# Filling products of ones in front of waits of TensorE, in a two-layer hybrid backbone on one NeuronCore

## What is computed

```python
# layer 0, state-space heads: both directions, chunkwise scan with scalar decay
y, ss_f, ss_b = bidir_scan(ch, bh * dt[0], bh * dt[1], xh, log_a[0], log_a[1], init[2], init[3])
y = y + xh * d_skip[None, :, None, None]
y = y.transpose(0, 2, 1, 3).reshape(b, l, SSD_INNER) * jax.nn.silu(z)
y = rmsnorm(...)                               # then concatenated, @ w_out
# layer 1, mLSTM
den = jnp.sum(s, axis=-1) + w_inter * jnp.einsum('bhid,bhd->bhi', qc, n0)
h = num / jnp.maximum(jnp.abs(den), jnp.exp(-m_row))[..., None]
```

## Time and profile before

| | us |
|---|---|
| median of 3 runs | 2368.23 |
| lowest and highest of them | 2364.69, 2372.87 |
| the profiled execution | 2359.82 |
| its span, first to last instruction | 2358.1 |
| busy in it: PE, DVE, ACT, POOL | 2274.4, 1370.9, 905.6, 1058.7 |
| mean granted clock of TensorE | 0.987 |

### The profile page before, as it was taken

How to read it: one execution, slowest core, us unless ns; L and a number is a source line. 1 busy time by engine, 2 the same in 40 slices (tenths; PEclk the granted TensorE clock), 3 DMA queues, 4 the chain that set the end, 5 groups by cost and what they waited for, 6 DMA issues and landing times.

```text
span 2358.1 us, 32703 instructions
## 1 busy us (share of the span) xinstructions
PE 2274.4 (96%) x11907; PEld 1962.0 (83%) x11907; DVE 1370.9 (58%) x1750; ACT 905.6 (38%) x1979; POOL 1058.7 (45%) x815
## 2 busy tenths in 40 slices
PE   7999999999879999999999999999999999999998
PEld 5999999998537999999999998976555568888887
DVE  5995788764666456856857456653568654111113
ACT  5215435443793256756746252132221213101002
POOL 3353334334541445534544434455133145866664
PEclk9999999999898999999999999999999999999999
DMA  7953334254540234434434423454233213333332
GB/s 274 310 163 115 103 110 144 83 178 140 185 127 26 65 99 123 146 106 125 144 107 125 84 78 120 131 178 133 62 113 96 68 46 91 97 98 98 98 96 83
DMA packets 392724, 281.07 MB, mean 119 GB/s; under 512 B 33442, under 2 KB 357820, under 8 KB 392604
## 3 DMA queue, kind: packets, MB, share of 16 engines
q1 hardware_dynamic: 333420, 200.46, 28.7%
q10 hardware_dynamic: 59184, 78.99, 9.8%
HBM read 237.34 MB, written 42.07 MB: 118 GB/s over the span
## 4 chain that ended last, share of the span: by engine, by line
PE 63%; DVE 4%; ACT 2%; DMA 1%; issue 1%; POOL 0%; ACTq 0%; DVEq 0%; POOLq 0%; SPq 0%
PE PS L961 46%; PE PS L1651 4%; PE PS L1480 3%; PE PS L1492 3%; PE PS L1603 2%; PE PS L1302 1%; DVE xcr L2499 1%; PE PS L1552 1%; DMA xmr<-xm_d 1%; PE PS L1429 0%; PE PS L899 0%; PE PS L893 0%; DVE hh L3074 0%; PE PS L1571 0%; DVE hh L3072 0%
## 5 line engine op out<-in xcount | busy, mean ns | idle before, releaser
L961 PE MATMUL PS<-act_hi,w_hi 128*128 128x384 f32 (+1 forms) x1824 | 637.8, 350 | 7.6 <-ACT act_hi L2100 2.8
L961 PE MATMUL PS<-act_hi,w_lo 128*128 128x384 f32 (+1 forms) x1824 | 630.1, 345 | 0.0
L961 PE MATMUL PS<-act_lo,w_hi 128*128 128x384 f32 (+1 forms) x1824 | 627.2, 346 | 0.0
L743 POOL TENSOR_TENSOR w_hi<-w_raw,ones 128x128 fp32r<-128x128 f32 x232 | 133.6, 576 | 1064.1 <-DMA w_raw<-in_ffn_w 404.9
L746 POOL TENSOR_TENSOR w_lo<-w_raw,w_hi 128x1024 fp32r<-128x1024 f32 (+1 forms) x232 | 558.5, 2407 | 19.3
L961 PEld LDWEIGHTS PS<-act_hi,w_hi 128*128 128x128 f32 x1824 | 343.0, 188 | 30.1 <-issue 13.4
L961 PEld LDWEIGHTS PS<-act_lo,w_hi 128*128 128x128 f32 x1824 | 343.7, 189 | 15.1 <-issue 1.2
L961 PEld LDWEIGHTS PS<-act_hi,w_lo 128*128 128x128 f32 x1824 | 343.0, 188 | 13.7
L2115 ACT ACTIVATE fprod<-mf_ring,cs 128x128 f32<-128x128 f32 x896 | 267.9, 388 | 26.4 <-DVE mf_acc L2414 26.4
L2414 DVE TENSOR_REDUCE mf_acc<-fprod 128x128 f32<-128x1024 f32 x112 | 224.9, 2020 | 85.8 <-ACT fprod L2115 85.8
L744 POOL TENSOR_SCALAR w_hi<-w_raw 128x896 fp32r<-128x896 f32 (+1 forms) x232 | 233.8, 1008 | 0.0
(11 more groups left out here) (376 smaller groups left out, 3684.6 us busy)
## 6 DMA issues: line engine op xcount, KB each, us to landing
w_raw<-in_ffn_w SPq DMA_DIRECT2D x120, 512.0 KB, 3.9
mf_ring<-in_w_mod SPq DMA_DIRECT2D x56, 512.0 KB, 3.7
w_raw<-in_a_w_in SPq DMA_DIRECT2D x44, 512.0 KB, 4.1
proj<-stage ACTq DMA_DIRECT2D x44, 384.0 KB, 4.2
w_raw<-in_b_w_up SPq DMA_DIRECT2D x32, 512.0 KB, 4.5
m_ring<-in_w_mod SPq DMA_DIRECT2D x12, 1024.0 KB, 9.1
rows<-g_d SPq DMA_DIRECT2D x16, 768.0 KB
m_raw<-in_w_mod SPq DMA_DIRECT2D x4, 2048.0 KB, 12.3
```

The costliest lines, as they stand in the source:

```text
L743: pool.tensor_tensor(w_hi[:, s, 0], w_raw[:, s, 0], ones[:], ALU.mult)
L961: last = pe.matmul(to[:, c0:c1], w[:, s, k, :], x[:, k, c0:c1], start=k == 0 and w is w_hi and x is hi, stop=k == kt - 1 and w is w_lo)
```

## The change

A helper `spare_products(at, n)` multiplies the ones n times into 128 columns of PSUM from column `at`. It is called: five times n = 5 in `x_transposes(p)` for p = 3 to 7, ahead of the wait for the tile's DMA, which is moved behind the function's other waits; six times n = 5 in `pair_products(p)` for p = 2 to 7, ahead of the skip products; four times n = 4 ahead of `context_decays(2p+2)` for p = 2, 4, 5 and 6, behind a wait for `y_done` that the pair has later anyway; once n = 6 ahead of the projection `out1`; and four products stand ahead of each mLSTM head's wait for `den_rdy`. In all 93 products: 25 + 30 + 16 + 6 + 16. Nothing reads them, and nothing else changes.

```diff
@@ -1229,8 +1229,12 @@
                         last = pe.transpose(bank(6)[:, (6 * d + c) * 32:(6 * d + c) * 32 + 32], r_nb[:, d, c * P:c * P + P], ident[0:32, 0:32])
                 last.then_inc(ct_mm, 1)
 
+            def spare_products(at, n):
+
+                for _ in range(n):
+                    pe.matmul(PS[:, at:at + P], ones[:], ones[:], start=True, stop=True)
+
             def x_transposes(p):
-                pe.wait_ge(xt_in[p % 3], 16 * (p // 3 + 1))
                 if p == 0:
                     pe.wait_ge(ct_put, 1)
                     pe.wait_ge(cb_put, 7)
@@ -1240,6 +1244,9 @@
                     pe.wait_ge(evac, segs["out1"][0])
                 if p == 5:
                     pe.wait_ge(cb_put, 14)
+                if p >= 3:
+                    spare_products(4096 - P, 5)
+                pe.wait_ge(xt_in[p % 3], 16 * (p // 3 + 1))
                 for c in range(6):
                     last = pe.transpose(slot(3)[:, c * P:c * P + P], xt[p % 3][:, c * P:c * P + P], ident[:])
                 last.then_inc(xt_tr, 1)
@@ -1291,6 +1298,7 @@
                 pe.wait_ge(skip_put, p + 1)
                 if p >= 2:
                     pe.wait_ge(y_done, p - 1)
+                    spare_products(1024 * (p % 2), 5)
                 for c0, c1 in ((0, LAT), (LAT, T)):
                     pe.matmul(y[:, c0:c1], skip[:, p % 2], xt[p % 3][:, c0:c1], start=True, stop=False)
                 pe.wait_ge(m_done, 2 * p + 2)
@@ -1321,6 +1329,9 @@
                 elif p + 1 < PAIRS:
                     if p == 1:
                         x_transposes(2)
+                    if p >= 2:
+                        pe.wait_ge(y_done, p - 1)
+                        spare_products(1024 * (p % 2), 4)
                     context_decays(2 * p + 2)
                 if p + 1 == PAIRS:
                     first_sums()
@@ -1347,6 +1358,7 @@
             n0 = segs["out1"][0]
             pe.wait_ge(w_split, n0 + 3)
             pe.wait_ge(y_done, PAIRS - 1)
+            spare_products(0, 6)
             pe.wait_ge(nhi_done, READY["ssd"] + 1)
             second_out_products(0, ((w_hi, act_hi), (w_lo, act_hi)))
             pe.wait_ge(act_ready, READY["ssd"] + 1)
@@ -1628,6 +1640,8 @@
                 else:
                     first_out_tile(3)
                     first_out_tile(4)
+                for _ in range(4):
+                    pe.matmul(bank(0, P), ones[:], ones[:], start=True, stop=True)
                 pe.wait_ge(den_rdy, DEN_RDY0 + h + 1)
                 for d in range(2):
                     for c in range(4):
```

## The result

The change makes the kernel slower: a median of 2374.46 us in 13 executions, against 2364.69 us for the kernel before in 13, and by the ratio of the two 1.0048 (95% interval 1.0036 to 1.0060), which is 11.4 us (8.5 to 14.2). The same kernel on another occasion gave 1.0037 (1.0025 to 1.0049), 8.8 us. The forecast was 2371.4 us, within 2363 to 2378.5: the sign and the range held, and the amount, 3.2 us, was a little over a quarter of what was measured.

What follows compares the result with a forecast made beforehand. The last-ending chain lay on PE for 63% of the span, but ACT set the pace in the pairs. Terms summed to +1.7 us, plus 1.5 for a returning half clock: 2368.23 + 3.2 = 2371.4 us, range 2363 to 2378.5.

Steps and rivals of the forecast that it cites:

- Who waits for whom: State-space pairs, 626 to 717 us: ACT sets the pace, PE follows; 4.5 us of clock at pair 6 give 0.6.
- What a product costs: Anywhere PE is the one waited for: 0.235 us per product; nothing where a wait as long covers it.
- Which are covered: Waits cover products at pairs 2, 4 to 6, the projection and nearly all at head 3; 22 uncovered cost 5.2 us.
- The half clock behind the projection's wait: Projection behind the pairs, 734 to 737 us: half clock goes, -1.5 us, and 0 if it doesn't.
- The half clock behind head 3: Behind head 3's denominators, 1884 to 1887 us: if the half clock goes, -1.5 us, on the path.
- The half clock at pair 7: New wait of about 2.7 us ahead of pair 7: one half-clock stretch of 3.0 us comes back, +1.5 us.
- that gives nothing: Pair 2: the half clock of 639 to 651 us may go, without gain, as ACT is busy throughout.
- The term that was mis-sized: Pair 3: ten products, ahead of skip products and transposes, delay DVE, POOL and ACT; +2.4 us, not given back.
- the prediction's sum: Whole kernel: 2.4 - 0.6 - 1.5 + 2.8 + 0.1 - 1.5 = +1.7 us, plus 1.5 for a returning half clock: +3.2.
- the four stretches that the prediction names: Half clock at 639 to 651, 707 to 716, 734 to 737 and 1884 to 1887 us.
- The base: Time the forecast starts from: median 2368.23 us, 8.4 us above the profiled execution's 2359.82.

Runs made afterwards that it cites:

- e8: The kernel before, run once more unchanged for a second trace, against the kernel before: 0.9998 (0.9985 to 1.0010), -0.5 us.
- e4: Kernel before plus the change without pair 3's ten products, pair 7's five ahead of its skip products and the mLSTM's, against the kernel before: 0.9999, -0.2 us.
- e5: As e4, plus five products ahead of pair 7's skip products, against the kernel before: 0.9989 (0.9976 to 1.0003), -2.6 us.
- e2: Kernel before plus only four products ahead of each mLSTM denominator, against the kernel before: 0.9994 (0.9981 to 1.0007), -1.4 us.
- e10: Only products lying in waits: those of e5 and four ahead of head 3's denominators, against the kernel before: 0.9999 (0.9983 to 1.0015), -0.2 us.
- e11: As e2, with eight products ahead of each mLSTM denominator instead of four, against the kernel before: 1.0015 (1.0000 to 1.0030), +3.5 us.
- e1: The change without the four products ahead of each mLSTM denominator, against the kernel before: 1.0034 (1.0016 to 1.0052), +8.0 us.
- e6: The whole change without the ten products at pair 3, against the kernel before: 1.0012 (1.0000 to 1.0025), +2.8 us.
- e7: The changed kernel, run once more for a second trace, against the kernel before: 1.0037 (1.0025 to 1.0049), +8.8 us.
- e9: As e3, with ten products at each of pair 3's two places, 20 in all, against the kernel before: 1.0055 (1.0036 to 1.0074), +13.0 us.
- e12: The kernel of e3, run once more, against the kernel before: 1.0033 (1.0015 to 1.0050), +7.8 us.
- e3: Kernel before plus only pair 3's ten products, five ahead of the skip products and five ahead of the transposes: 1.0016 (0.9999 to 1.0032), +3.8 us.

## Why the prediction was right, and where it was too small

*Who waits for whom.* The reading that ACT sets the pace of the pairs was right. The half clocks over pairs 2 and 6, 21 us of them in the trace before, went and gave 0.5 us where PE won 4.5 at pair 6 alone, as forecast (0.6). Over the `Dm` products of pair 6 a half clock stood in none of the seven traces with products there and in six of the seven without; over those of pair 2 in none and in four. One more half clock of that trace, over pair 4's skip products (2.93 us for four records at 675.89 us, 1.46 after), wasn't named in the prediction. It cost nothing: from the end of the score products to pair 4's `Dm` it is 14.84 us with it and 14.83 in e8 without.

*What a product costs.* 0.235 us was right: 2.27 us for ten where 2.4 were forecast, 0.89 at head 0. By the Trainium skill (TensorE: Matmul & The Clock Gate, Back-to-back issue gap), 81 ns for each of the two records, an estimate would have been 1.6 us for the ten; the traces don't agree with it.

*Which are covered.* Right at pairs 2, 4, 5, 6 and 7 and at the projection (e4 and e5 show no cost). Right that ten at pair 3 and twelve at heads 0 to 2 are not.

*The half clock behind the projection's wait.* Right in size (1.55 us, forecast 1.5). It was gone in all seven traces with the six products, and there in six of the seven without, so the products do hold the clock here. As a gain it should have been 1.5 us times the share of executions that have it.

*The half clock behind head 3.* Wrong for the change: it is still there in both traces of it, since PE's wait behind the four products (1.73 us in the first) is longer than the one they filled. With products there it was gone in three of six traces (e2, e10 and, with eight products, e11), without in one of eight. So of that term about half a microsecond is left.

*The half clock at pair 7.* The forecast put 1.5 us for a fall that comes back there. The mechanism and the place were right, and the size was 1.0: behind the wait of 2.5 to 3.6 us ahead of pair 7 the clock was at 0.50 over its products in five of the seven traces with the pairs' products (e1, e5, e6, e7, e10; 12.0 to 12.2 us to the projection against 11.2), and in e8. The first trace of the change is one of the two without.

*What it overlooked ahead of pair 3.* I had worked through pair 2 and stopped at "that gives nothing"; the question of what is late next wasn't asked there. In ten of the 14 traces PE waits 2.7 to 3.6 us ahead of the score products, in all seven with products at pair 2 and in three without (e8, e9, e12). The clock fell in nine of these ten waits, and in four (the first of the change, e5, e8, e10) it stayed down long enough that the products took 9.2 to 9.3 us and not 7.95. That is 1.3 us in three of the seven traces with the products, and in one of the seven without.

*The term that was mis-sized* is pair 3's. Its 2.4 us are in the trace, but the kernel loses 5.8 (e3, e12) to 6.0 us (change against e6) by these ten products, and 13.0 by twenty. In the timed executions the rest goes with the clock. On one chip the mean granted clock was 0.98644 in the kernel before, 0.98367 with the ten (e12) and 0.98300 with the twenty (e9). Times the kernel's length that is 6.6 us (95% interval 2.5 to 11.1) and 8.1 us (4.3 to 12.4) of lost clock, a part of which may lie where nobody waits for PE. With the 2.3 and 4.5 us of the products' own length it comes near the 7.8 and 13.0 us measured. On another chip it was 0.9900 in e6 and 0.9889 in the change, 2.6 us (0.1 to 5.2) of the 3.7 that are missing there. On e3's chip it can't be told: 0.9838 against 0.9845, with one execution of the kernel before at 0.938. Where in the kernel that is can be seen in part. The stretch from the first norm product of the second layer to the last one at the end of the kernel holds the same work in all 14 traces, but for the products of ones ahead of the denominators. Its two ends in four kernels (before, e5, the change, e12), timelines of PE. Before:

```profile
1369.27 1.47 PE L893 MATMUL PS<-ones,nacc 128*128 128x1 f32 x12 [0.51 <-DVEq L2453]
...
2349.02 1.02 PE L893 MATMUL PS<-ones,nacc 128*128 128x1 f32 x8 [1.14 <-DVEq L3085]
```

979.8 us. With what lies in waits (e5):

```profile
1373.82 1.47 PE L893 MATMUL PS<-ones,nacc 128*128 128x1 f32 x12 [0.63 <-DVEq L2464]
...
2353.14 1.02 PE L893 MATMUL PS<-ones,nacc 128*128 128x1 f32 x8 [1.14 <-DVEq L3096]
```

979.3 us. The change:

```profile
1375.70 1.47 PE L893 MATMUL PS<-ones,nacc 128*128 128x1 f32 x12 [0.69 <-DVEq L2467]
...
2367.02 1.02 PE L893 MATMUL PS<-ones,nacc 128*128 128x1 f32 x8 [1.14 <-DVEq L3099]
```

991.3 us. Only pair 3's ten (e12):

```profile
1374.61 1.47 PE L893 MATMUL PS<-ones,nacc 128*128 128x1 f32 x12 [0.69 <-DVEq L2460]
...
2366.74 1.02 PE L893 MATMUL PS<-ones,nacc 128*128 128x1 f32 x8 [1.14 <-DVEq L3092]
```

992.1 us, with no product of ones added anywhere in it. With the price of the products in the heads taken off (2.9 us for four, 5.6 for eight), the six traces of kernels with products at pair 3 (the change twice, e1, e3, e9, e12) have 986.0 to 992.1 us, mean 989.1; the eight without have 978.3 to 982.1 us and, in the kernel before run again, 986.9: mean 981.0. Added up over the same stretch, the clock was at 0.50 for 20.5 us on average in the six and 10.7 us in the eight, which is 5 us of the 8. The stretch from the start to the pairs, which nothing touches, comes out alike in both, 607.9 and 607.8 us. But the 8 is too large as a price: the six profiled executions lay on average 2.6 us above the medians of their kernels, and the eight 0.7 us below, so some 3 us of it are which executions happened to be profiled.

Almost half of the difference, 3.7 us, lies ahead of head 0's denominators, and the traces differ there in one place, 55 us into the stretch. PE's timelines there, in the change and in e5:

```profile
1430.63 0.74 PE L1426 MATMUL PS<-bdT 128*128 128x128 f32 x2 [2.65 <-ACT bdT L2189]
```

```profile
1428.08 0.49 PE L1425 MATMUL PS<-bdT 128*128 128x128 f32 x2 [0.59 <-ACT bdT L2186]
```

All six traces have the long wait for ACT's `bdT`, and a half clock with it; of the eight, the two of the kernel before and e2 have the wait, and e8 and e2 the fall. From the norm product to head 0's denominators, less the price of the products in front of these, it is 282.2 to 283.9 us in the six, 283.6 and 281.8 in e8 and e2, and 277.4 to 279.3 in the other six. Neither the wait nor the fall needs a product at pair 3, but both were there each time that it had some.

*A DVE operation at head 3* is a second loss that the prediction didn't have, and it isn't pair 3's. From head 2's denominators to head 3's it takes 80.0 us in the two traces of the change, in e1 and in e6, and 77.4 to 79.1 in all others. These are the four traces in which DVE's last sum ahead of head 3 took 2.8 us (last section). With the sizes above, and each fall times its share of the traces, the prediction's sum comes to 2.3 - 0.5 - 1.3 + 2.7 - 0.5 + 0.7 + 0.6 = 4.0 us, an estimate (the 0.6 is the score products' 1.3 in three of seven traces); with 1.9 us for this operation (80.0 against 78.1 in e2) to about 6. What is missing to the 8.8 and 11.4 us measured is about what pair 3's ten lose above their length.

So a delay at pair 3 goes with more half clock several hundred us later, in work that is the same. Why isn't settled. The clock falls at a given wait in one execution and not in another, so where in time the wait comes may matter, and a delay moves every later wait. That would explain a difference of either sign; why it is a loss on average in the timed runs of e9, e12, e1 and the change isn't shown. The Trainium skill (TensorE: Matmul & The Clock Gate, Part 1) states that what watches the activity runs freely against the kernel; the two traces of the kernel before agree with it, as behind the same wait of 2.81 us the clock fell in one and not in the other. It was in the prediction, used to halve the gains, and should have been used on everything behind the change as well. The trace before had 61 us at half clock (0.987 over 2358.1 us), and the four stretches that the prediction names make up only half of them.

*The base.* I used 2368.23 us, the median of 3; over 13 executions the kernel before has 2364.69. With the latter the same sum would have given 2367.9 us, 6.6 us below what was measured. That the forecast of 2371.4 came within 3.1 us is in part luck: a base 3.5 us too high made up for half of it.

## What to carry to other kernels

Before filling a wait to hold a clock, ask who waits for the engine whose clock it is: here PE got 21 us of half clock back beside a busy ScalarE, and the kernel got half a microsecond. A filling product is free only if its whole length lies in the wait and stays there once the clock is up; ten uncovered ones, 2.3 us long, cost the kernel about 6, and the other 83 gave nothing that could be measured. And where a clock changes in some executions and not in others, compare the same stretch of work across several traces, with and without, before putting a number to a fall. The mean granted clock of all timed executions says more of it than any one trace.

## What was not expected of the hardware

DVE's sum of 128x512 elements, 0.69 us long at heads 1 and 2 in every trace, took 1.31 us at head 3 in the trace before and 2.81 in the trace after. On POOL's timeline after:

```profile
1893.44 2.35 POOL L746 TENSOR_TENSOR w_lo<-w_raw,w_hi 128x1024 fp32r<-128x1024 f32 x1
```

It runs from 1893.44 to 1895.79 us, and DVE's two-operand operation that started at 1893.52 ended at 1896.33, half a microsecond behind it. Before, POOL's same operation started at 1881.33, when DVE's, started at 1880.48, was two thirds through.

The 14 traces hold 280 such sums. Without a POOL operation beside them, 252 took 0.68 or 0.69 us. Of the 14 beside one with a single tensor as input (at head 0, where POOL's starts and ends are rough), 13 did, and one took 1.07. The 14 at head 3 ran beside a POOL operation with two inputs, and were the longer the longer the two ran together: 0.69 us with 0.06 together (e5), 0.83 and 0.84 with 0.3 (e8, e9, e11), 1.30 and 1.31 with 0.46 (the trace before, e2, e3, e4, e10, e12), and 2.80 and 2.81 with 2.26 (both of the change, e1, e6). In these last four POOL had started 0.09 us ahead of DVE, in the six before them 0.85 us behind. So one POOL operation with two inputs can hold a DVE one up for its whole length, and the order of the two is decided by less than a microsecond. No run here moves one against the other on purpose.
